# Experts as 16 pairs of 64-row slots, one expert's weights on each column half of the array

## The reference

```python
def hier_moe(xn, p):
    shp = xn.shape
    z = xn.reshape(-1, shp[-1])
    pg = jax.nn.softmax((z @ p['router_gw'] + p['router_gb']).astype(F32), axis=-1)
    gw, gsel = lax.top_k(pg, 1)
    ...
    tv, ti = lax.top_k(le_sel, TOP_FINE)
    fine = jnp.einsum('nk,nke->ne', jax.nn.softmax(tv, axis=-1), jax.nn.one_hot(ti, EXP_PER_GROUP, dtype=F32))
    comb = ((gw * gsel_1h)[:, :, None] * fine[:, None, :]).reshape(-1, N_EXPERTS)
    hg = jnp.einsum('nd,edf->nef', z, p['exp_w_gate'])
    hu = jnp.einsum('nd,edf->nef', z, p['exp_w_up'])
    h = jax.nn.silu(hg) * hu * comb[:, :, None].astype(z.dtype)
    return jnp.einsum('nef,efd->nd', h, p['exp_w_down']).reshape(shp)
```

## Time and profile before

| | us |
|---|---|
| median of three runs | 1448.09 |
| lowest and highest run | 1445.62, 1453.89 |
| span of the profiled execution | 1445.5 |
| TensorE busy in it | 1202.1 (83%) |
| experts' first gate-up matmul to the last down matmul's end | 1133.1 to 1411.5 |

### The profile page before, as it was taken

One profiled execution on the slowest core, in us unless ns is written; L12 is line 12 of the kernel. 1 busy time (PEld: TensorE's weight loads), 2 busy tenths in 40 slices (PEclk: granted clock), 3 DMA queues, 4 the chain that ended last, 5 costly groups with the idle time before them and its releaser, 6 DMA issues. The chain is left out here.

```text
span 1445.5 us, 24975 instructions
## 1 busy us (share of the span) xinstructions
PE 1202.1 (83%) x8815; PEld 888.9 (61%) x8815; DVE 588.9 (41%) x1648; ACT 400.6 (28%) x887; POOL 223.9 (15%) x353
## 2 busy tenths in 40 slices
PE   5899996295799589998999957979797799999990
PEld 4799995252655477776777734978585444454440
DVE  3733346537377213343433435465247211121115
ACT  1300003521177224334443421023314111111112
POOL 2000000000300435523355000000000111111113
PEclk9999998556599789999999956999997899999995
DMA  6144442600780896769788352214254266655515
GB/s 188 30 87 87 120 119 81 207 1 3 223 316 1 174 209 169 206 182 222 206 222 217 101 164 63 73 44 171 86 207 178 77 248 241 238 213 199 204 44 192
DMA packets 180245, 217.20 MB, mean 150 GB/s; under 512 B 78136, under 2 KB 150824, under 8 KB 173048
## 3 DMA queue, kind: packets, MB, share of 16 engines
q1 hardware_dynamic: 152440, 156.37, 35.3%
q0 software_dynamic: 23584, 57.48, 13.0%
q10 hardware_dynamic: 4128, 2.10, 0.8%
HBM read 218.94 MB, written 39.37 MB: 179 GB/s over the span
## 5 line engine op out<-in xcount | busy, mean ns | idle before, releaser
L2797 PE MATMUL bank<-wgu,memtok 128*128 128x512 f32 x384 | 170.5, 597 | 1.8 <-DVE memtok L3015 1.8
L2797 PEld LDWEIGHTS bank<-wgu,memtok 128*128 128x128 f32 x384 | 73.4, 192 | 94.3 <-issue 94.3
L1400 POOL DMA_DIRECT2D rawc<-in_cache_nsa_kv x128 | 75.2, 588 | 151.9 <-PE bank L1831 132.2
L2819 PE MATMUL bank<-wdn,yT 128*128 128x512 f32 x192 | 86.5, 593 | 1.5 <-DVE yT L3020 0.9
L1706 DVE COPY ZTs<-bank 128x512 f32<-128x512 f32 x64 | 44.2, 690 | 101.9 <-PE bank L1759 101.9
L265 PE MATMUL bank<-h_high,w_low 128*128 128x272 f32 x384 | 81.1, 293 | 5.2 <-DVE h_low L381 3.0
L265 PE MATMUL bank<-h_high,w_high 128*128 128x272 f32 x384 | 80.7, 292 | 0.0
L265 PE MATMUL bank<-h_low,w_high 128*128 128x272 f32 x384 | 80.3, 291 | 0.0
L3020 DVE COPY yT<-bank 128x256 f32<-128x256 f32 x24 | 10.2, 424 | 148.3 <-PE bank L2807 148.3
L265 PE MATMUL bank<-n_high,w_low 128*128 128x272 f32 x256 | 56.0, 301 | 14.7 <-DVE n_low L381 8.1
L1400 POOL DMA_DIRECT2D ring<-in_cache_nsa_kv x112 | 65.7, 587 | 14.3 <-issue 7.4
(11 more groups left out here) (586 smaller groups left out, 2312.9 us busy)
## 6 DMA issues: line engine op xcount, KB each, us to landing
kv<-in_cache_nsa_kv SPq DMA_DIRECT2D x256, 128.0 KB, 3.8
wgu<-in_exp_w_gate SPq DMA_DIRECT2D x24, 1024.0 KB, 4.8
wgu<-in_exp_w_up SPq DMA_DIRECT2D x24, 1024.0 KB, 7.1
wdn<-in_exp_w_down SPq DMA_DIRECT2D x24, 1024.0 KB, 4.9
rawc<-in_cache_nsa_kv POOLq DMA_DIRECT2D x128, 128.0 KB, 3.8
ring<-in_cache_nsa_kv POOLq DMA_DIRECT2D x112, 128.0 KB, 3.0
rows_dram<-zrow POOLq DMA_DIRECT2D x24, 512.0 KB, 18.6
ring<-in_w_in SPq DMA_DIRECT2D x44, 256.0 KB, 3.6
```

Source lines behind the costliest of these rows:

```text
L1400: return eng.dma_start(dst[64 * half:64 * half + 64, :, :, :].rearrange("p a c n -> p a (c n)"), cache[bass.ds(page, 1), :, :, kinds, :].r ...
L2797: mm = pe.matmul(gemm_big[n % 2][:, :].rearrange("p (m f) -> p m f", m=2), XT[:, n % 2, k, :], w[:, :, k, :], start=(k == 0), stop=(k == K ...
L2819: mm = pe.matmul(gemm_small[half][:, :], hT[:, n % 2, j, :], wdn[:, n % 3, at:at + 512], start=(j == 0), stop=(j == 1))
```

## The change

A slot now has 64 rows (`SL`), and there are 32 of them: one for each expert and 16 late ones (`NOV`). They are put in 16 pairs. The gathered rows of a pair lie in partitions 0 to 63 and 64 to 127 of one tile. The transposes stay as they were. In `gate_up` and `down` each matmul of 128 stationary columns becomes two of 64 columns, with the same 512 moving columns each but from different weights; they write partitions 0 to 63 and 64 to 127 of the same PSUM bank. There are four weight buffers, two for each pair; the fourth lies in `xn_tok`, which is free after the tokens' rows are stored.

```diff
-NOV = (2 * NT) // (P + 1)
+SL = 64
+NOV = (2 * NT) // (SL + 1)
 NSL = NE + NOV
+NPR = NSL // 2
+LOADS = [0, 1, 2]
+for _n in range(NOV):
+    LOADS += [NE + _n // 2 + (NOV // 2 if _n % 2 else 0)] + [_e for _e in (3 + _n,) if _e < NE]
+PAIRS = [LOADS[0:2]] + [[LOADS[2 * _p], LOADS[2 * _p + 1]] for _p in range(1, NPR)]
...
-                    for s in range(NSL):
+                    for s in range(NSL * SL // P):
                         pool.dma_start(rows_dram[P * s:P * s + P, :], zrow[:, :]).then_inc(zeroed, 16)
...
+            WR = 4
-            wdn = ctx.enter_context(nc.sbuf_tensor("wdn", [P, 3, 2 * D], F32, side="right"))
+            wdn = ctx.enter_context(nc.sbuf_tensor("wdn", [P, WR, 2 * D], F32, side="right"))
...
+            gain = x_flat[:, 0:D]
+            fourth = xn_tok[:, :, :].rearrange("p q n -> p (q n)")[:, 0:2 * KT * FF].rearrange("p (m n) -> p m n", m=2)
+            def gate_up_at(j):
+                return fourth if j == WR - 1 else wgu[:, j, :, :]
...
-                        if n >= 3:
-                            sp.wait_ge(gu_mm, n - 2)
-                            load_gate_up(sp, n % 3, e, used[slot - NE] if late_slot else None)
-                            sp.wait_ge(y_mm, n - 2)
-                            load_down(sp, n % 3, e, used[slot - NE] if late_slot else None)
+                        if s < WR:
+                            sp.wait_ge(xn_saved, 16 * NQ)
+                        else:
+                            sp.wait_ge(gu_mm, (s - WR) // 2 + 1)
+                        load_gate_up(sp, gate_up_at(s % WR), s % WR, e, cond)
+                        if s >= WR:
+                            sp.wait_ge(y_mm, (s - WR) // 2 + 1)
+                        load_down(sp, s % WR, e, cond)
+                        if s == WR:
+                            sp.wait_ge(tk_out, 4 * NQ)
+                            sp.dma_start(gain[:, :], I["final_norm"].rearrange("(a n) -> a n", a=1).to_broadcast([P, D]))\
                                .then_inc(gain_here, 16)
...
                     def gate_up(n):
-                        pe.wait_ge(gu_here[n % 3], 32 * (n // 3 + 1))
+                        for j in range(2):
+                            pe.wait_ge(gu_here[(2 * n + j) % WR], 32 * (2 * n // WR + 1))
...
                         for k in range(KT):
-                            mm = pe.matmul(gemm_big[n % 2][:, :].rearrange("p (m f) -> p m f", m=2), XT[:, n % 2, k, :],
-                                           w[:, :, k, :], start=(k == 0), stop=(k == KT - 1))
+                            for j in range(2):
+                                half = slice(SL * j, SL * j + SL)
+                                mm = pe.matmul(gemm_big[n % 2][half, :].rearrange("p (m f) -> p m f", m=2),
+                                               XT[:, n % 2, k, half], w[j][:, :, k, :],
+                                               start=(k == 0), stop=(k == KT - 1))
...
-                    for n in range(NSL):
+                    for n in range(NPR):
                         gate_up(n)
```

More of the change, by code:

```diff
@@ L2565, in _ @@
                     for j in range(3):
-                        load_gate_up(sp, j, slots[j])
-                        load_down(sp, j, slots[j])
+                        load_gate_up(sp, wgu[:, j, :, :], j, LOADS[j])
+                        load_down(sp, j, LOADS[j])
                 @block.tensor
@@ L2673, in _ @@
                     expert = None
-                    for n, slot in enumerate(slots):
+                    for s, slot in enumerate(LOADS):
+                        if s < WR - 1:
+                            continue
                         if slot >= NE and expert is None:
@@ L2810, in down @@
                     def down(n):
-                        pe.wait_ge(dn_here[n % 3], 16 * (n // 3 + 1))
+                        for j in range(2):
+                            pe.wait_ge(dn_here[(2 * n + j) % WR], 16 * (2 * n // WR + 1))
                         pe.wait_ge(ht_out, n + 1)
@@ L2816, in down @@
                         for half in range(2):
[L2817 to L2820, removed]
+                            for i in range(2):
+                                at = D * i + 512 * half
+                                for j in range(2):
+                                    rows = slice(SL * j, SL * j + SL)
+                                    mm = pe.matmul(gemm_small[half][rows, :], hT[:, n % 2, i, rows],
+                                                   wdn[:, (2 * n + j) % WR, at:at + 512], start=(i == 0), stop=(i == 1))
                         mm.then_inc(y_mm, 1)
@@ L2938, in _ @@
                     dve.wait_ge(rank_mm, 1)
[L2939 to L2942, removed]
+                    more = (NT - 1) // SL
+                    c.step(dve.tensor_tensor(late[:, 0:more, :], total.unsqueeze(1).to_broadcast([P, more, NE]),
+                                             slot_const("rowof")[:, 1:more + 1].unsqueeze(2).to_broadcast([P, more, NE]),
+                                             ALU.is_gt))
+                    c.step(dve.tensor_reduce(over, late[:, 0:more, :].rearrange("p m e -> p e m"), AX, ALU.add))
                     c.step(dve.tensor_tensor_scan(upto, const("ones")[:, 0:NE], over, 0.0, ALU.mult, ALU.add))
                     c.step(dve.tensor_tensor(start, upto, over, ALU.subtract))
[L2945 removed]
+                    c.step(dve.scalar_tensor_tensor(out=start, in0=start, scalar=float(SL), in1=slot_const("late0"),
                                                     op0=ALU.mult, op1=ALU.add))
                     c.step(dve.scalar_tensor_tensor(
[L2948 removed]
+                        out=dst[:, 0, :, :], in0=rank.rearrange("p (q e) -> p q e", q=NQ), scalar=SL - 0.5,
                         in1=start.unsqueeze(1).to_broadcast([P, NQ, NE]), op0=ALU.is_gt, op1=ALU.mult))
```

111 lines of the change are left out of this document (49 added, 62 removed).

## The result

| | us |
|---|---|
| before, median of 13 runs (lowest, highest) | 1448.07 (1443.54, 1459.99) |
| changed, median of 13 runs (lowest, highest) | 1456.02 (1451.82, 1467.34) |
| ratio, with its 95% interval | 1.0056 (1.0033 to 1.0079) |
| span of the profiled execution, changed | 1451.3 (before 1445.5) |
| experts' stage in it, first gate-up to the last `down`'s end | 1130.25 to 1417.26, 287.0 (before 278.3) |

The change makes the kernel slower by 8 us, which is 0.6%; the interval is 4.8 to 11.4 us. 1456 was forecast.

The account below looks back on a forecast made before the run. The prediction took the experts' stage to be bound by TensorE, slot after slot. Its terms, -91.4 + 3.2 + 73.5 + 13.2 + 9.6 + 0.2 = +8.3 us, added to the median 1448.1 gave 1456 us, range 1440 to 1471.

Parts of the forecast that it names:

- (a): Experts' stage: 24 slots become 16 turns of 11.43 us, the two halves running side by side; -91.4 us.
- (b): TensorE going in and out of column halves: 0.2 us a turn over 16 turns; +3.2 us (0 to 6.4).
- (c): Odd pairs 3 to 13: TensorE waits 12.25 us each for the second slot's late-issued gate and up; +73.5 us.
- (d): Gate-ups behind the six long waits run partly at the lower clock, 2.2 us each; +13.2 us (10 to 19).
- (e): Small waits at even pairs and pair 15, from skipped issues behind the first slot's down load; +9.6 us (6 to 14).
- (f): Head of the stage and the rest: SyncE's longer reads, VectorE's instructions, fewer zero stores; +0.2 us (-1 to +2).
- TensorE stays the bound: Rival: the second slot's gate and up are not late, so waits and their clock loss go; 1360 us, chance 0.05.
- Waits at their lower bound: Rival: the six long waits take 10.3 us each with no loss of clock; 1431 us, chance 0.05.
- Weight loads bare: Rival: the halves' weight loads are not hidden, 24 steps of 0.137 us a turn; +53, 1509 us, chance 0.03.
- one after another: Rival: the halves' matmuls in gate-up and down do not overlap; +165, 1621 us, chance 0.02.
- More late slots: Rival: experts 3 or 11 exceed 64 rows, so pair 2's or 15's wait becomes full; up to 1469 us, chance 0.05.

Follow-up runs that it names:

- the repeat: The kernel before the change, profiled once more with nothing changed: 1446.1 us (1 run).
- halves in turn: Changed kernel with all matmuls of the first half issued before those of the second, in gate_up and in each bank of down: 1542.8 us.
- full-width work: Changed kernel with one matmul over 128 columns and the first slot's weights instead of two; loads, waits and turns stay: 1450.7 us, ratio 1.003.
- a turn's lead: Changed kernel with gate and up of both slots of a pair issued ahead of the previous pair's down loads: 1382.6 us, ratio 0.957.
- fillers: Changed kernel with twelve more full-width matmuls, into a bank nothing reads, before the gate-ups of pairs 3, 5, ..., 13: 1444.6 us, ratio 0.998.
- without the late loads: Changed kernel, same order of issue, with the weight loads of late slots 17 to 22 left out: 1375.9 us (1 run).
- the version without late bytes and a turn ahead: Changed kernel with both slots' gate and up ahead of the previous pair's down loads, and late slots 17 to 22 not loaded: 1361.2 us.
- the versions a turn ahead: Changed kernel with both slots' gate and up before the previous pair's down loads: 1382.6 us; also with three extra matmuls before gate-ups 5, 7, 11: 1379.7 us.

## Why the prediction was right

The forecast was 1456, the sum +8.3 us; measured are +8.0 in the medians and +8.7 in the stage of the two profiles. By its steps, where the last row but one is a cost that the prediction did not have:

| term | forecast | measured | from |
|---|---|---|---|
| (a) fewer turns | -91.4 | -91.4 | halves side by side; 11.43 a turn again in the repeat |
| (b) in and out of the halves | +3.2 | +5.6 | 16 x 0.35 |
| (c) six long waits | +73.5 | +71.2 | 11.22 to 12.34 each |
| (d) clock behind them | +13.2 | +11.6 | excess of the odd pairs' gate-ups over 7.09 in the chain |
| (e) small waits | +9.6 | +8.6 | 0.71 to 1.50 each |
| around each wait, beyond its length | 0 | +3.2 | 14 x 0.23 |
| sum, stage | +8.1 | +8.8 | 287.0 - 278.3 = 8.7 |

The agreement of the sums to 1 us is in part luck: (b) and the cost around the waits were 5.6 us too low together, and (c), (d) and (e) 4.9 us too high. The mechanism and each term's size within about 3 us are not luck.

(a) held. The rows of lines 1034 and 1037 were a good witness: there as here two streams with weights of their own run at once. The halves in turn show that it depends on the alternation in the gate-up.

(b) was mis-sized, within its bounds: 0.35 us a turn for 0.2. From the start of each piece to the start of the next, 0.11 of it is in the gate-up (6.97 for 6.86), 0.10 in the two transposes behind it (0.33 for 0.23), 0.09 in the eight behind those and 0.05 in `down`.

(c) was right in mechanism and number, and 2.3 us too large; two of the waits (11.43 and 11.22) lie below the 11.5 to 13 that was named as its sign. The 0.2 us that I had added stand for SyncE's reaction to `down`'s end and TensorE's to the landing, and lie inside the wait; the first is 0.05 (1166.57 to 1166.62). What the sum lacked is a cost outside it: 0.25 a turn in full-width work, 0.22 in halves (12.00 minus 11.78). The order of issue was the cause, shown in three steps: 3.1 us less a wait with one transfer moved back, 37.6 us in place of 71.2 with the loads ahead of the wait for `down`, 10 us with a turn's lead.

(d) was right in mechanism and 12% too large. The six excesses are 1.5, 2.6, 1.4, 3.0, 1.7 and 1.4 us. They spread more than the sign said: gate-ups of 8.7 to 9.3 us were named, and only one of the six (8.83) lies there, though the mean is 9.02. The fillers take five of the excesses away at once.

(e) held, 1.0 us below. That these waits are too short to change the clock held too: the gate-ups behind them took 7.09 us. Pair 12 waited 1.34 us where the other even ones waited 1.01. SyncE's two skipped issues stand 0.50 us apart there (1349.52 and 1350.02) and 0.20 at pair 8; without the late loads the same pair waited 1.33. Why stays open.

(f) can't be told from scatter. Two statements of the prediction were a little off and change nothing: the bounds of (a) to (f) add up to 1434 and 1478, not 1438 and 1472, and the earlier trace rows show a copy late twice (0.9 us each, at the stage's ends), where the text has none late. The lead of 2.9 us at the stage's start is why the spans differ by 5.8 us only, while the stage has grown by 8.7.

Of the rivals, "TensorE stays the bound" was priced at 1360; the version without late bytes and a turn ahead, at 1361, is that case, but the changed kernel's order of issue does not allow it. "Waits at their lower bound" (1431) would have had 10.3 us and no loss of clock; the shortest was 11.22, and each was followed by a slow gate-up. "Weight loads bare" (1509) and "one after another" (1621) fall with the profile: 32 records in 7.02 us. The Trainium skill's page "TensorE: Matmul & The Clock Gate", Part 3 (Packing small matmuls), would have had the loads wait by the sentence that the prediction drew on, as the two halves share their row group; the trace disagrees with it. The same section also lets a load go ahead of running matmuls when it goes to the background weight buffer, and with that the trace agrees, though no run here shows where the loads go. In the halves' gate-ups from 1182 to 1200 the loads last 132 to 137 ns, 16 steps of them would be 2.2 us, and the whole gate-up is 0.16 us longer than before. The serial rival's 165 us is the price of no overlap at all; the nearest order tried, one half's gate-up matmuls all ahead of the other's, cost 86. "More late slots" did not occur: the waits of pairs 2 and 15 are 1.50 and 0.71.

## What to carry to other kernels

A queue that issues in order gives each transfer the wait of everything ahead of it. If buffers of two kinds come free at different times, the load that is needed first must not stand behind the wait for the buffer that comes free last; here the order alone moved the ratio from 1.0056 to 0.957. And when a change puts two slots into one turn, both slots' loads have one turn's time to hide in: count what must be issued and landed in one turn before counting the turns saved.

## What had not been expected of the hardware

- Two column halves overlap only over a short reach. With all 16 records of one half ahead of the other's, only four of each ran side by side; a gate-up took 12.3 us against 7.1. The second half's first record started ahead of the first half's last three, which stand before it in the program (1156.33 against 1156.75 and later).
- A wait costs TensorE 0.22 to 0.25 us beyond its own length: the end of the work ahead of it and the first step behind it are longer (`down` 3.65 to its modelled end instead of 3.48 to the next start, gate-up 7.02 instead of 6.97).
- Behind column halves, full-width transposes take longer at first: 0.33 us instead of 0.23 for the two right behind the gate-up.
- The clock did not follow the length of a wait alone. In the versions a turn ahead the gate-up took 7.09 us behind a wait of 2.25 us, 8.78 behind 2.83, 10.04 behind 3.13, and again only 8.78 behind 4.18; behind the waits of 12 us it took from 8.5 to 10.0. In the changed kernel with fillers two waits of 2.02 us were followed by 8.79 (pair 7) and 7.09 (pair 11). So a wait of 3.13 us, a quarter of those priced in (d), can cost as much of the clock as the longest of them; what decides it was not tried.
- The 16 DMA engines were full (a share of 0.97 to 1.02) at 387 to 426 GB/s (387 in the version a turn ahead from 1218, 426 in the changed kernel from 1218 to 1222). It did not slow TensorE's own steps: in the version a turn ahead, within the 140 us at 397 GB/s, a gate-up without a wait before it (from 1177.19) took 6.96 us, as in the one without late bytes.
